# Two gated merges with a PSUM operand in every VectorE operation, transposes through the accumulator banks, and xT at another address

## The reference, cut to what matters

```python
# block 1
gates = sigmoid(g.reshape(B, S, 3, D) + b_gate)
merged = (gates[:, :, 0] * (merge_heads(o_m) @ w_br_moba)
          + gates[:, :, 1] * (merge_heads(o_d) @ w_br_diff)
          + gates[:, :, 2] * (merge_heads(o_s) @ w_br_sb))
x = layer_norm(alpha * x + merged @ w_out)
# block 2: the same with two branches (w_a2d, w_b2d), sigmoid gates and w_o
```

## Time and profile before

| | |
|---|---|
| median of 3 runs | 1271.55 us (1266.17 to 1272.37) |
| the profiled execution, its own time | 1267.03 us |
| its span | 1265.2 us |
| PE, POOL, ACT, DVE busy | 91%, 72%, 49%, 40% |
| first merge: transposes to the last `mT` slice | 418.5 to 471.2 us |
| second merge: transposes to the last `mT` slice | 962.3 to 1003.6 us |

### The profile page before, as it was taken

How to read it: one execution, slowest core, us unless ns; L and a number is a source line. 1 busy time by engine, 2 the same in 40 slices (tenths; PEclk the granted TensorE clock), 3 DMA queues, 4 the chain that set the end, 5 groups by cost and what they waited for, 6 DMA issues and landing times.

```text
span 1265.2 us, 22521 instructions
## 1 busy us (share of the span) xinstructions
PE 1155.6 (91%) x8040; PEld 1071.9 (85%) x8040; DVE 508.5 (40%) x986; ACT 617.2 (49%) x970; POOL 912.2 (72%) x700
## 2 busy tenths in 40 slices
PE   6999997998999898999995998699897979999985
PEld 6999996997889777999995987599877879999964
DVE  4111117003345789211116536442467743433452
ACT  5443444445557634344434764523355375545554
POOL 7899995996544686999994886735223959899973
PEclk9999998999999998999997998999998989999988
DMA  8865563665332354665654454422122635665641
GB/s 296 275 185 183 183 190 107 188 196 150 117 101 81 115 161 128 201 185 193 183 184 133 149 185 134 150 64 88 50 67 65 194 117 183 185 182 186 192 137 50
DMA packets 52630, 193.39 MB, mean 153 GB/s; under 512 B 5840, under 2 KB 6096, under 8 KB 51920
## 3 DMA queue, kind: packets, MB, share of 16 engines
q1 hardware_dynamic: 50976, 184.57, 47.1%
q10 hardware_dynamic: 1584, 7.81, 1.8%
HBM read 191.31 MB, written 1.05 MB: 152 GB/s over the span
## 4 chain that ended last, share of the span: by engine, by line
POOL 42%; PE 27%; issue 22%; DVE 6%; ACT 2%; POOLq 1%; DMA 0%; ACTq 0%; DVEq 0%; SPq 0%
POOL weights_low L482 42%; PE banks L513 15%; PE acc L513 7%; PE banks L873 3%; DVE mT_low L1511 1%; DVE mT_high L1535 1%; ACT tmp L1205 1%; DVE tmp L1876 0%; DVE tmp L1878 0%; PE banks L706 0%; ACT prob L1104 0%; POOLq L485 0%; DVE xs L1505 0%; DVE xs L1499 0%; DVE nmx L1553 0%
## 5 line engine op out<-in xcount | busy, mean ns | idle before, releaser
L482 POOL TENSOR_TENSOR weights_low<-ring,weights_high 128x512 fp32r<-128x512 f32 x696 | 911.9, 1338 | 332.7 <-ACT weights_high L998 329.0
L513 PE MATMUL banks<-xT_high,weights_high 128*128 128x256 f32 x1680 | 483.1, 288 | 21.8 <-POOL weights_low L482 10.9
L998 ACT CAST weights_high<-ring 128x1024 fp32r<-128x1024 f32 x348 | 361.1, 1047 | 276.9 <-PE banks L513 204.6
L513 PE MATMUL banks<-xT_high,weights_low 128*128 128x256 f32 x1680 | 480.4, 286 | 0.0
L513 PE MATMUL banks<-xT_low,weights_high 128*128 128x256 f32 x1680 | 479.9, 286 | 0.0
L513 PEld LDWEIGHTS banks<-xT_high,weights_high 128*128 128x128 f32 x1680 | 324.4, 193 | 27.1 <-issue 11.9
L513 PEld LDWEIGHTS banks<-xT_low,weights_high 128*128 128x128 f32 x1680 | 323.4, 192 | 2.6
L513 PEld LDWEIGHTS banks<-xT_high,weights_low 128*128 128x128 f32 x1680 | 322.1, 192 | 0.0
L1386 DVE TENSOR_TENSOR hf<-act_buf,banks 128x256 f32<-128x256 f32 x44 | 18.5, 421 | 286.8 <-ACT act_buf L1024 286.7
L513 PE MATMUL acc<-weights_high,hT_high 128*128 128x512 f32 x264 | 104.0, 394 | 3.9 <-DVE hT_low L1395 3.9
L513 PE MATMUL acc<-weights_high,hT_low 128*128 128x512 f32 x264 | 104.4, 396 | 0.0
(11 more groups left out here) (317 smaller groups left out, 1485.9 us busy)
## 6 DMA issues: line engine op xcount, KB each, us to landing
ring<-in_stream SPq DMA_DIRECT2D x348, 512.0 KB, 3.6
rows<-in_big_rows ACTq DMA_DIRECT2D x3, 1024.0 KB, 7.2
rows<-in_big_rows ACTq DMA_DIRECT2D x3, 512.0 KB, 4.2
cst<-in_consts ACTq DMA_DIRECT2D x1, 1411.0 KB, 9.1
gates<-in_x_fm SPq DMA_DIRECT2D x2, 512.0 KB, 5.4
xs<-in_x_tm ACTq DMA_DIRECT2D x1, 1024.0 KB, 5.9
out<-xs SPq DMA_DIRECT2D x4, 256.0 KB, 2.0
pT<-in_p_fm ACTq DMA_DIRECT2D x1, 256.0 KB, 2.8
```

The source lines that it names most:

```text
L482: last = nc.gpsimd.tensor_tensor(wlo[:, slot, hs], ring[:, slot, hs], whi[:, slot, hs].bitcast(F32), ALU.subtract)
L513: ins = nc.tensor.matmul(o, lhsT, rhs, start=start, stop=stop, **kw)
L998: nc.scalar.copy(whi[:, ch % RING, :], ring[:, ch % RING, :]).then_inc(S["hi_ready"], 1)
```

## The change

The gated products and sums are rearranged so that every DVE operation of a merge reads PSUM: the two-branch product is written in place into its PSUM bank, the last sum is written into PSUM too, ACT makes `mT_high` from there, and DVE subtracts for `mT_low` one slice later. A bank of `branch n.b` or `mix n` is thus freed by the low part (`merged`, `mixed`). The one long sigmoid becomes one per branch and two slices (12 of 512 columns in the first merge, 8 in the second), placed among ACT's weight casts. The transposes of `o1` and of the two outputs go to `acc` banks: in the first merge three of five run before the last two sb outputs and the other two between `branch0.a` and `branch0.b`; in the second, the parts of the output that is ready first are transposed first. The normalization on DVE moves ahead of the subtraction of the running sums, and gate projections 17 to 23 run half a step later each, so that one stands in step 8. Two filler tiles are added: 88 floats ahead of `xT` and 168 ahead of `hT`. `oT_high` and others change places, with starts that are the same as before past a multiple of 1024 bytes.

```diff
-    return (16 + first + half,) if first < 8 else ()
+    return (16 + first + half - (first > 0),) if (first, half) not in ((0, 1), (8, 1)) else ()
...
+        sb("fill_x", [88])
         xT = pair("xT", [KD, T])
...
+        sb("fill_stage", [168])
         hT = pair("hT", [GROUP, T], in_ffn)
...
# PE
             def turn_o(k):
-                o = take(f"oT{k}")
+                if k == 0:
+                    pe.wait_ge(S["acc_read"], 4)
+                if k == 4:
+                    pe.wait_ge(S["oT_ready"], 1)
...
+                if first == H1 + 2:
+                    pe.wait_ge(S["o_normed"], 1)
+                    for k in range(3):
+                        turn_o(k)
                 for h in sb_heads(first - 4):
...
-            pe.wait_ge(S["oT_ready"], 5)
+            pe.wait_ge(S["oT_ready"], 3)
             for n in range(8):
                 o = take(f"branch{n}.a")
...
+                if n == 0:
+                    pe.wait_ge(S["sb_out"], H1)
+                    turn_o(3)
+                    turn_o(4)
+                    pe.wait_ge(S["oT_ready"], 5)
...
+            pe.wait_ge(S["attn_out"], N_INST1 + N_INST2)
+            turn_y(2)
+            turn_y(3)
+            pe.wait_ge(S["gdn_normed"], 1)
+            turn_y(0)
+            turn_y(1)
# ACT, first merge (the second is alike, and there the load of p_raw is waited for after slice 0)
-            nc.scalar.activation(g1, g1, ACT.Sigmoid).then_inc(S["gates_ready"], 1)
+            for n in range(8):
+                if n % 2 == 0:
+                    for b in range(3):
+                        g1 = gates1[:, b, n:n + 2, :].rearrange("p a t -> p (a t)")
+                        nc.scalar.activation(g1, g1, ACT.Sigmoid).then_inc(S["gates_ready"], 1)
+                feed(jobs[index[f"branch{n}.b"]][2])
+                act.wait_ge(S["summed"], n + 1)
+                nc.scalar.copy(mT1[0][:, n, :], bank(f"branch{n}.b")[:, 0:T]).then_inc(S["merged_high"], 1)
# DVE, first merge
+                v.tensor_tensor(pair_a, gates1[:, 0:2, n, :], pair_a, ALU.mult)
                 job_wait(dve, f"branch{n}.b")
+                part = tmp[:, n % 2, 0:T]
+                link(v.tensor_tensor(part, gates1[:, 2, n, :], tb[:, 0:T], ALU.mult))
+                link(v.tensor_tensor(part, part, ta[:, 0:T], ALU.add))
+                v.tensor_tensor(tb[:, 0:T], part, ta[:, T:2 * T], ALU.add).then_inc(S["summed"], 1)
+                if n:
+                    merged_low(mT1, n - 1, bank(f"branch{n - 1}.b"), "merged", 0)
# DVE, second merge
+                v.tensor_tensor(part, gates2[:, 0, n, :], tile[:, 0:T], ALU.mult)
+                link(v.tensor_tensor(tile[:, T:2 * T], gates2[:, 1, n, :], tile[:, T:2 * T], ALU.mult))
+                v.tensor_tensor(tile[:, 0:T], part, tile[:, T:2 * T], ALU.add).then_inc(S["summed"], 1)
```

More of the change, by code:

```diff
@@ L166, in job_table @@
             job(f"sbo{h}", ("sb_out", h + 1))
-    for k in range(5):
-        job(f"oT{k}", ("oT_ready", k + 1))
     for n in range(8):
-        job(f"branch{n}.a", ("branch_a", n + 1), blocks=6)
-        job(f"branch{n}.b", ("branch_b", n + 1), blocks=3)
+        job(f"branch{n}.a", ("summed", n + 1), blocks=6)
+        job(f"branch{n}.b", ("merged", n + 1), blocks=3)
     pos[0] = PART_AT["ffn1"]
@@ L235, in job_table @@
             job(f"gmix{12 + i}", ("gmix_raw", 13 + i), blocks=8)
-    for k in range(4):
-        job(f"yT{k}", ("yT_ready", k + 1))
     for n in range(8):
-        job(f"mix{n}", ("mix_gated", n + 1), blocks=8)
+        job(f"mix{n}", ("mixed", n + 1), blocks=8)
     pos[0] = PART_AT["ple"] + 16
@@ L936, in _, with turn_y @@
                     project_fm(f"gmix{12 + i}", xT)
[L937 to L940, removed]
+            def turn_y(k):
                 src = og if k < 2 else o2
-                if k == 2:
-                    pe.wait_ge(S["attn_out"], N_INST1 + N_INST2)
                 for kk in range(2):
@@ L1162, in _, with high_o @@
                     gate_raw(i)
+            def high_o(k):
+                n = 2 if k < 4 else 1
+                act.wait_ge(S["oT_turned"], k + 1)
+                nc.scalar.copy(oT[0][:, 2 * k:2 * k + n, :].rearrange("p a t -> p (a t)"), acc[:, k % 4, 0:n * T]
+                               ).then_inc(S["oT_high"], 1)
             for first in range(0, H1 + 4, 2):
@@ L1179, in _ @@
                     gate_raw(i)
+                if first == H1 + 2:
+                    for k in range(3):
+                        high_o(k)
                 if first == H1 - 2:
@@ L1183, in _ @@
                                          ).then_inc(S["subln_std"], 1)
[L1184 to L1188, removed]
-            act.wait_ge(S["gate_raw"], 24)
-            g1 = gates1[:].rearrange("p a b t -> p (a b t)")
-            nc.scalar.activation(g1, g1, ACT.Sigmoid).then_inc(S["gates_ready"], 1)
+            warm(ACT.Sigmoid)
+            high_o(3)
+            high_o(4)
+            act.wait_ge(S["gate_raw"], 24)
+            for n in range(8):
[6 more added lines that the diff above has]
+                nc.scalar.copy(mT1[0][:, n, :], bank(f"branch{n}.b")[:, 0:T]).then_inc(S["merged_high"], 1)
             feed_to(PART_AT["ffn1"] // CB + 1)
@@ L1319, in _ @@
                                  ).then_inc(S["gdn_std"], 1)
+            warm(ACT.Sigmoid)
             act.wait_ge(S["gmix_raw"], 16)
-            g2 = gates2[:].rearrange("p a b t -> p (a b t)")
-            nc.scalar.activation(g2, g2, ACT.Sigmoid).then_inc(S["gmix_ready"], 1)
-            for k in range(4):
-                wait_job(f"yT{k}")
-                nc.scalar.copy(yT[0][:, 2 * k:2 * k + 2, :].rearrange("p a t -> p (a t)"), bank(f"yT{k}")).then_inc(S["yT_high"], 1)
+            for i, k in enumerate((2, 3, 0, 1)):
+                act.wait_ge(S["yT_turned"], i + 1)
+                nc.scalar.copy(yT[0][:, 2 * k:2 * k + 2, :].rearrange("p a t -> p (a t)"), acc[:, k, :]).then_inc(S["yT_high"], 1)
             act.dma_start(p_raw, p_fm).then_inc(S["p_in"], 16)
-            act.wait_ge(S["p_in"], 16)
-            nc.scalar.copy(pE[0][:], p_raw).then_inc(S["x_high"], 1)
             rows_in(4)
+            for n in range(8):
+                if n % 2 == 0:
+                    for b in range(2):
+                        g2 = gates2[:, b, n:n + 2, :].rearrange("p a t -> p (a t)")
+                        nc.scalar.activation(g2, g2, ACT.Sigmoid).then_inc(S["gmix_ready"], 1)
+                feed(jobs[index[f"mix{n}"]][2])
+                act.wait_ge(S["summed"], 8 + n + 1)
+                nc.scalar.copy(mT2[0][:, n, :], bank(f"mix{n}")[:, 0:T]).then_inc(S["merged_high"], 1)
+                if n == 0:
+                    act.wait_ge(S["p_in"], 16)
+                    nc.scalar.copy(pE[0][:], p_raw).then_inc(S["x_high"], 1)
             feed(PART_AT["ple"])
```

96 lines of the change are left out of this document (48 added, 48 removed).

## The result

Four runs of the changed kernel took 1254.16 to 1257.29 us, median **1255.63**, against 1270.65 for four of the kernel before: a ratio of 0.9887 (95% interval 0.9858 to 0.9917). It is faster, as forecast, but by 15 us where 41 were forecast, and outside the range that ended at 1248.

What follows compares the result with a forecast made beforehand. The prediction took PE to set the pace in the feed-forward parts and projections, and DVE in the merges. Its terms, 29 + 1 + 8.5 + 2.7 = 41.2 us, came off the median 1271.55 to give 1230 us, range 1216 to 1248.

Steps and rivals of the forecast that it cites:

- A: Feed-forward parts and projections: new address makes matmuls with xT moving 6.4 ns faster; 29 us, bounds 0 and 33.
- B: Value and small projections, last into_acc: 336 matmuls with xT stationary gain from the address; 1 us, bounds 0 and 2.2.
- C: Start of the first merge: branch products begin at 420.6 to 422.1 against 422.64; 8.5 us together with D.
- D: First merge's slices: DVE (2.5 us) and ACT (2.6) fit under PE's 3.06, PE becomes the bound; 8.5 with C.
- ACT's sigmoids: First merge: 1.5 sigmoids of 512 columns a slice at 0.45 us each, within ACT's 2.6 us.
- The stall by the early normalization: Ahead of the first merge: ACT's exps and PE wait behind DVE's moved normalization; 1 to 1.5 us.
- The stop before `branch0.b`: First merge: two more transpose jobs, a copy and a subtraction interrupt PE's branch products; 2.3 us.
- E: Second merge: starts near 965.2 instead of 967.10 and a wait of 0.82 goes; 2.7 us, bounds 0 and 3.5.
- step 6: Where PE waited in step 6: a granted clock at the lower level, listed as a sign of being wrong; no size.
- The address does what it was said to do: Rival, for xT's matmuls: the address does nothing, only 11.2 us are gained, 1260 us; chance 0.12.
- PSUM writes are cheap: Rival, in both merges: DVE operations writing PSUM cost 1.38 us, giving 1248 us; chance 0.05.
- 960 is good for xT: Rival, for xT's matmuls: the new place is worse, one more step of 6.4 ns, 1292 us; chance 0.03.

Runs made afterwards that it cites:

- e1_addr_only: The kernel before with the two filler tiles alone, so only addresses move; 1250.55 us, ratio 0.9896.
- e5_both: The changed kernel with four gate projections spread over block 2's attention steps and the merges' sigmoids issued one slice earlier; 1247.84 us.
- e12_fill: e5_both with two of the spread projections moved into PE's waits ahead of block 2's attention, the others at attention steps 5 and 11; 1240.54 us.
- e3_gmix_spread: The changed kernel with four gate projections at attention steps 1, 5, 9, 13 of block 2 in place of 0 to 3; 1245.93 us, ratio 0.9820.
- the merges alone: The changed kernel without the two filler tiles, so xT lies where it lay before; 1264.74 us, ratio 0.9974.
- e14_addr_again: The kernel of e1_addr_only run again, unchanged, to count runs with the long stretch; 1253.07 us.
- e8: e5_both with other filler sizes, so xT begins 992 bytes past a multiple of 1024; 1261.30 us.
- e9: e5_both with other filler sizes, so xT begins 704 bytes past a multiple of 1024; 1246.40 us.
- e15: e12_fill with DVE's normalization back behind the subtractions, as in the kernel before; 1242.77 us, ratio 0.9772.

## Why the prediction failed, point by point

The forecast was 41.2 us, profile to profile it is 12.8: 28.4 short.

**A and B, forecast 30, measured 24.** The mechanism held to the number: 113.8 ns for the 113.4 taken, 8.21 us a step for 8.19, POOL not the bound. That all three parts of the profile had the faster of the two paces was partly luck: 29 of 36 parts had it, and the changed kernel's other profile has one at 8.42, 4.2 us longer. The three parts and the first steps gave 17.4 where 66 steps by 0.31 were 20.3, as a few steps at the start and at the end of a part were held up and ran 8.3 to 8.7. The projections gave 6.7 of 12, because from 300 to 360 us they ran at 117.8 ns, a mean pace that no stretch of before had, and partly under the waits that I had put at 3. B has no price of its own: into the last w products at xT the distance between starts went from 234.3 to 233.3 ns (229.0 in e1_addr_only), in the value projections from 173.3 to 173.6.

**C and D, forecast 8.5, measured 4.8.** Two terms were mis-sized, and both experiments give them back. I had counted ACT's sigmoids as busy time (2.6 us a slice against 3.06) and not as a link: they stand behind the copy of slice n-1, which waits for `summed`, and DVE's next product waits for them. I also took 0.45 us for one of 512 columns from the long one; it is 0.63 (row below). That cost 2.8 us. The stall by the early normalization was put at 1 to 1.5 us; ACT waited 2.85, and undoing it brings 1.3. With both mended the first merge gains 4.8 + 2.8 + 1.3 = 8.9 of 8.5. The group of the sigmoids in the branch products:

```profile
L1211 ACT ACTIVATE gates<-gates 128x512 f32<-128x512 f32 x12 | 6.7, 628 | 0.0
```

The stop before `branch0.b` was forecast at 2.3 us and took 2.5 between starts.

**E, forecast 2.7.** The start gained 1.51 (forecast 1.9) and the wait behind it 1.10 (0.8): 2.6. The `mix` products had no stop, but their first 5 us fell into the lower clock, which took 2.4 of it back. That isn't the long stretch's doing alone: the `mix` products take 24.2 us in e5_both and 23.2 in e12_fill, which don't have it but have a short fall that reaches into them. In the kernel before, the short fall at the end of the attention was over 2 us before they began.

**The step that failed is one that isn't in the sum.** I priced every stretch at the clock that the trace of before shows in it, and for the clock wrote down only that it might fall in step 6. In the attention of block 2, where the diff touches nothing, it cost 15.3 us: 1.9 for a short fall that e1_addr_only has too, 13.4 for the long stretch. This and the 2.4 are 17.7 of the 28.4 missing. The rest is A and B with 5.9, C and D with 3.7, E with 0.1 and the end of the kernel with 1.0. Without the 17.7 the time would have been 1238, inside the range; that is a sum and not a run. e3_gmix_spread, without the long stretch but with short falls in the same part, took 1245.93.

**The rivals.** None came. The address does what it was said to do, PSUM writes are cheap, 960 is good for xT. By the formula of the Trainium skill, "TensorE: Matmul & The Clock Gate", "Wait — 56ns, not 53.3ns?", which the prediction cites, a matmul would start every 109 ns, an estimate; the best pace in these traces is 113.4, so the formula doesn't give the pace here at either address. The Trainium skill, "TensorE: Matmul & The Clock Gate", "What's actually happening", says that the lower clock is the default and activity releases it. The trace agrees as far as the falls go: in the changed kernel's profile each begins in a wait of PE of 0.5 us or more, or at most 2.0 us behind one, the long one too (0.88 us). It doesn't show the release: PE was busy for 18 of 18 us at the lower level, and the clock stayed there. For the next forecast, the thin matmuls of this attention keep the upper clock in most runs of before, and did not bring it back in 51 us once it had fallen.

**What stays open.** Why the changed kernel falls into the stretch every time and the address alone in one run of three. The banks are excluded, and so is the faster pace, since the merges alone have it too. PE's instructions are the same in both from 877 us on, and up to 908 us their distances agree within 0.05 us. Then, at the first attention step without a projection, PE waits longer for ACT's exps in the changed kernel than with the address alone:

```profile
909.59 0.52 PE L704 MATMUL banks<-cst,prob 128*128 128x128 f32 x3 [0.88 <-ACT prob L1113]
```

```profile
916.44 0.52 PE L708 MATMUL banks<-cst,prob 128*128 128x128 f32 x3 [0.52 <-ACT prob L1106]
```

All six profiles with the long stretch have the longer wait (1.25 us between starts), and the clock falls 1.2 to 2.0 us behind it; the three of before and of the address alone have 0.90 and don't fall there. The wait is longer because DVE starts on the scores 1.37 us after PE's first matmul for them in place of 1.02, and the profile shows nothing that DVE waited for. That this wait tips the clock is not shown: no run changed it alone, and the runs of the address alone that have the stretch weren't profiled. The point in time at which this part begins differs too, by the microseconds that each kernel saves; a kernel that changes this alone was not run either.

## What to carry to other kernels

A speed-up moves everything behind it, and a part that keeps its clock by a narrow margin can lose it: look through the kernel for long parts with small matmuls, and price them at both levels in the range, even where nothing in them changes. Spreading dense matmuls through such a part is a cheap guard (9.7 us between medians here for moving four projections), as long as no long wait is left uncovered where they stood (4.16 us in e12_fill). When an engine's work is cut into pieces and put between another engine's steps, follow one whole cycle of waits through it; that its busy time fits isn't enough.

## What was not expected of the hardware

The SBUF address of the moving operand sets the pace of the 128x256 matmuls: 119.5 to 119.9 ns at remainder 0 modulo 128 and at 608, 118.3 at 672 and at 992, 113.4 to 113.9 or 117.8 at 64 modulo 128. At the good addresses the pace has two values and keeps one for tens of microseconds; in e14_addr_again it changed behind a step that took 0.2 us more. `yT`, at 960 in every kernel, has the two values as well: its products ran at 113.4 ns in most profiles, the one of before among them, and at 117.8 in e3, e8, e9, e14 and e15. The prediction took its 113.4 from one profile that showed the better value. One stretch at the lower clock also splits the runs of one kernel into two groups: 1272 to 1277 against 1261 to 1265 us for the merges alone, where the profiled run of the first group shows it, and by the clock 1279 against 1268 for the kernel before.
